# Cached keys of the sliding heads: one transfer of 512 KB for each chunk of four sequences

## Time and profile before

| what | value |
|---|---|
| median of 3 runs | 3058.83 us (3041.25 to 3075.09) |
| profiled execution, its own time | 3047.57 us |
| its span, from first to last instruction | 3045.9 us |
| PE busy | 2879.0 us, 95% of the span |
| PEld busy | 2334.0 us, 77% |
| DVE busy | 1530.6 us, 50% |
| ACT busy | 604.9 us, 20% |
| POOL busy | 174.2 us, 6% |
| mean granted TensorE clock | 0.974 of full |

### The profile page before, as it was taken

One profiled execution on the slowest core, in us unless ns is written; L12 is line 12 of the kernel. 1 busy time (PEld: TensorE's weight loads), 2 busy tenths in 40 slices (PEclk: granted clock), 3 DMA queues, 4 the chain that ended last, 5 costly groups with the idle time before them and its releaser, 6 DMA issues.

```text
span 3045.9 us, 45683 instructions
## 1 busy us (share of the span) xinstructions
PE 2879.0 (95%) x16270; PEld 2334.0 (77%) x16270; DVE 1530.6 (50%) x3125; ACT 604.9 (20%) x1279; POOL 174.2 (6%) x207
## 2 busy tenths in 40 slices
PE   7999999999898899999989999999898989999997
PEld 5888887878765678888778888778786657888885
DVE  5444537746655254445354454485475632544534
ACT  1000001124464210010010000112335641000000
POOL 3000000000142000000000000000003310000000
PEclk9999999999999899999999999999998999999998
DMA  7532222230279523322233312222205793233122
GB/s 162 140 83 71 60 77 80 73 101 0 82 238 272 155 76 83 83 69 63 73 104 83 83 55 82 71 84 70 74 0 175 232 264 110 70 83 83 52 78 67
DMA packets 366185, 301.35 MB, mean 99 GB/s; under 512 B 14738, under 2 KB 338540, under 8 KB 365842
## 3 DMA queue, kind: packets, MB, share of 16 engines
q1 hardware_dynamic: 341756, 217.98, 25.7%
q0 software_dynamic: 24256, 81.11, 8.9%
HBM read 287.21 MB, written 14.45 MB: 99 GB/s over the span
## 4 chain that ended last, share of the span: by engine, by line
PE 87%; DMA 4%; DVE 4%; issue 2%; ACT 2%; DVEq 1%; SPq 0%; ACTq 0%; POOL 0%; POOLq 0%
PE banks L731 34%; PE banks L824 18%; PE banks L756 5%; PE banks L767 5%; PE banks L695 4%; PE banks L1412 4%; PE banks L895 2%; PE banks L906 2%; PE banks L1090 2%; PE banks L1078 2%; PE banks L1094 2%; DMA arena<-in_cache_v,layer_cache_rows 1%; DMA keys_values_by_token<-in_w_gate 1%; PE banks L1307 1%; PE banks L1243 1%
## 5 line engine op out<-in xcount | busy, mean ns | idle before, releaser
L731 PE MATMUL banks<-normed_or_mixed,arena 128*128 128x272 f32 x1408 | 337.8, 393 | 4.5 <-DVE arena L1976 4.5
L731 PE MATMUL banks<-arena 128*128 128x272 f32 x1408 | 337.0, 392 | 0.0
L731 PEld LDWEIGHTS banks<-normed_or_mixed,arena 128*128 128x128 f32 x1408 | 266.9, 190 | 62.5 <-issue 4.1
L731 PEld LDWEIGHTS banks<-arena 128*128 128x128 f32 x1408 | 267.5, 190 | 55.1
L731 PE MATMUL banks<-arena,keys_values_by_token 128*128 128x272 f32 x832 | 204.4, 392 | 0.0
L731 PEld LDWEIGHTS banks<-arena,keys_values_by_token 128*128 128x128 f32 x832 | 158.1, 190 | 32.6
L824 PE MATMUL banks<-hidden_or_projected,keys_values_by_token 128*128 128x272 f32 x704 | 177.0, 392 | 0.0
L824 PE MATMUL banks<-arena,keys_values_by_token 128*128 128x272 f32 x704 | 169.6, 393 | 1.0 <-DVE arena L2033 1.0
L1490 ACT ACTIVATE hidden_or_projected<-banks 128x1024 f32<-128x1024 f32 (+4 forms) x160 | 130.9, 827 | 199.4 <-PE banks L695 122.7
L824 PE MATMUL banks<-hidden_or_projected,weight_slots 128*128 128x272 f32 x704 | 169.2, 392 | 0.0
L1974 DVE TENSOR_TENSOR arena<-arena,banks 128x272 f32<-128x272 f32 x88 | 38.4, 437 | 236.4 <-PE banks L731 236.4
(11 more groups left out here) (392 smaller groups left out, 4466.3 us busy)
## 6 DMA issues: line engine op xcount, KB each, us to landing
weight_slots<-in_w_down SPq DMA_DIRECT2D x128, 256.0 KB
weight_slots<-in_w_in SPq DMA_DIRECT2D x28, 1024.0 KB
keys_values_by_token<-in_w_gate SPq DMA_DIRECT2D x48, 512.0 KB, 5.0
keys_values_by_token<-in_w_up SPq DMA_DIRECT2D x48, 512.0 KB, 5.2
weight_slots<-in_w_gate SPq DMA_DIRECT2D x40, 512.0 KB, 5.0
weight_slots<-in_w_up SPq DMA_DIRECT2D x40, 512.0 KB, 5.1
hidden_or_projected<-in_cache_win_k SPq DMA_DIRECT2D x112, 128.0 KB, 6.4
weight_slots<-in_w_down SPq DMA_DIRECT2D x64, 192.0 KB
```

The source lines that it names most:

```text
L731: mm = pe.matmul(ps[:, bank, 0:HALF], weights[:, k, :], acts[:, k, :], start=first and k == 0, stop=k == 3, skip_group_check=True)
```

## The change

The four requests of a chunk are written as one: the source is taken over four sequences at once, four sequences x 32 rows x 4 KB, and the destination is the whole slot, 128 partitions x 4 KB. It adds 16 to the semaphore once. The counts that the users of `bk_in` wait for go down accordingly from 64 to 16 for each chunk. Nothing else is touched: the order of the requests on SP, the waits before them, the ring and TensorE's program are as they were.

```diff
@@ -408,12 +408,12 @@
             chunks = (CH_B + RING - 1 - slot) // RING
-            return s[f"bk_in{slot}"], l * (64 * chunks + 32) + 64 * chunks + (32 if m > 8 else 16)
+            return s[f"bk_in{slot}"], l * (16 * chunks + 32) + 16 * chunks + (32 if m > 8 else 16)
 
         def b_keys_in(l, m):
 
             chunks = (CH_B + RING - 1 - m % RING) // RING
-            return l * (64 * chunks + 32) + 64 * (m // RING + 1)
+            return l * (16 * chunks + 32) + 16 * (m // RING + 1)
@@ -558,13 +558,13 @@
                     i, g, slot = m // 2, m % 2, m % RING
                     sp.wait_ge(s["k_free"], k_seen(l, CH_C + m))
                     alone(sp)
-                    for b4 in range(4):
-                        rows = A["cache_win_k"][ds(l, 1), 4 * g + b4].rearrange("l p h d -> (l p) (h d)")
-                        if i < 4:
-                            src = rows[1536 + 128 * i:1664 + 128 * i].rearrange("(k r) c -> k r c", r=4)
-                        else:
-                            src = rows[512 * (i - 4):512 * (i - 3)].rearrange("(k r) c -> k r c", r=16)[:, 0:4, :]
-                        ld(k_rows_in[32 * b4:32 * b4 + 32, slot], src, f"bk_in{slot}")
+                    rows = A["cache_win_k"][ds(l, 1), 4 * g:4 * g + 4].rearrange("l b p h d -> (l b) p (h d)")
+                    if i < 4:
+                        src = rows[:, 1536 + 128 * i:1664 + 128 * i].rearrange("b (k r) c -> b k (r c)", r=4)
+                    else:
+                        src = rows[:, 512 * (i - 4):512 * (i - 3)].rearrange("b (k r) c -> b k r c", r=16)[:, :, 0:4, :]\
+                            .rearrange("b k r c -> b k (r c)")
+                    ld(k_rows_in[:, slot].rearrange("p r c -> p (r c)"), src, f"bk_in{slot}")
                 for m in range(2 * NB_S):
```

## The result

Four runs of the changed kernel have a median of 3118.86 us (3116.65 to 3125.82) against 3053.63 us for four runs of the kernel before, a ratio of 1.0211 with a 95% interval of 1.0181 to 1.0240. The forecast was 3128, with a range of its own of 3105 to 3150. The two medians lie 65.2 us apart. The profiled execution has a span of 3116.7 us, 70.8 us more than before; the forecast for both was 69 more.

The account below looks back on a forecast made before the run. PE bounds the kernel (busy 95%), with DMA engines nearly without reserve in the key stage. Four engines carrying keys plus values add 34.5 us per layer, 69 in all, to the 3058.83 median: 3128 us, range 3085 to 3205.

Parts of the forecast that it names:

- What bounds it, and what could be won: Whole kernel and B's key stage: PE sets the pace, DMA share 0.99; a better load could return 10.6 us, 0.35%.
- The requests that go: SP's queue: 56 requests per layer become 14, freeing 13.3 us at 0.316 us each, worth nothing by itself.
- How the one transfer is dealt out: Joined key request: outermost counts 4 against 128 give four engines, the same each time, 128 KB on each.
- a table of 34 rows: Set-up load at 0.13 share, 2.1 engines, 55 GB/s; taken as evidence that engines get equal shares of the outermost count.
- What four engines can carry: Key stage: each engine moves 2.523 MB at 23.6 GB/s, 106.9 us, so 34.5 us more per layer, 69 in all.
- my upper pace: Key stage: at 26.4 GB/s per engine the bytes take 95.6 us, 23.2 us more per layer, 46 in all.
- PE's own work lies wholly inside, also where its clock falls: Key stage: PE's 64.89 us of work fits inside the 110 us, with 35 us more to spare at a lower clock.
- What would show it: Expected signs: key waits about 35 us per layer, value waits gone, SP's stretch towards 95 us, rate near 185 GB/s.
- All sixteen engines: Joined key request is cut by its 128 destination rows; at most 10.6 us gained, 3048 us; chance 0.10.
- The ring hides it: Key stage: four engines, but requests go out 10 to 16 us ahead; 5.4 us late per layer, 3070; chance 0.08.
- The slow pace: Key stage: four engines at 15.9 GB/s, from two queues or the 2 MB distance; up to 173 us, 3232; chance 0.17.

Follow-up runs that it names:

- `sixteen`: Changed kernel with its single 512 KB request reordered to (row, sequence), outermost count 32; 3042.95 us, ratio 0.9952 to the kernel before.
- `by_row`: Kernel before with each chunk's four 128 KB requests taking one 1 KB row of all 128 partitions, outermost count 4; 3127.61 us.
- `pairs`: Kernel before with a chunk's four requests joined two and two, 256 KB each, outermost count 2; 3264.32 us.
- `novals_after`: Changed kernel with the last sixteen requests for C's values in each layer left out; 3066.89 us, against 3021.33 for the kernel before cut likewise.
- `quarters`: Kernel before with partitions ordered (row, sequence): four requests per chunk, 8 rows x 4 sequences onto 32 partitions, eight engines; 3066.72 us.
- `halves`: Kernel before with partitions ordered (row, sequence): two requests per chunk, 16 rows x 4 sequences onto 64 partitions, sixteen engines; 3045.34 us.
- `by_pool`: Changed kernel with the same key request, outermost count 4, asked for by POOL between its requests for values; 3098.87 us, ratio 1.0141.

## Why the prediction was right

**What bounds it, and what could be won.** Right, as far as it can be told. The stage had no DMA engine to spare, and only waits of 10.6 us could be won. `sixteen` takes the waits for keys away and shortens the stretches by 1.1 and 0.6 us. Its timed gain of 0.5% is more, some 14 us, though its interval, 9 to 20 us, holds the 10.6. Where the rest comes from is in part open. The profiles show it outside the stretch (2885.4 against 2892.7 us), where single profiles differ as much by themselves, and there is one profile of each. The timed runs say what goes with it: their mean granted clock is 0.9775 in the median with `sixteen` and 0.973 before, and among the runs before alone the one at 0.975 took 3047.27 us and the one at 0.968 took 3067.07, which by estimate makes 13 us for a difference of 0.0045. Part of it is the stage itself (0.98 and 0.96 in place of 0.93, and 0.92 in place of 0.83 in the 33 to 35 us behind it in the first layer); what lifts the rest isn't shown.

**The requests that go.** The direction was right, the price off: one request of the new form takes SP 0.556 us and not 0.316, so that 14 of them save 56 x 0.316 - 14 x 0.556 = 9.9 us per layer and not 13.3. It is worth nothing, as forecast: `by_row` has all 56 requests and is as slow.

**How the one transfer is dealt out.** Right, and shown three ways: 4.2 engines in the window in which only keys move; count 4 against 32 at equal size and number; two engines with `pairs`. The guess by analogy from a table of 34 rows on 2.1 engines held. The Trainium skill, "DMA: Bandwidth & Descriptors", under "Why a DMA increments its semaphore by 16 and not by 1", has the rule and says the lowest-numbered engines are taken on SP's queue, while POOL's rotates. No run here shows an engine's number, but that the load adds up on SP's queue (share 0.58) and spreads on POOL's (0.92) agrees.

**What four engines can carry.** Right within 4 us. From the first request at 918.05 to chunk 45 at 1031.67, less 2.65, each of the four moved 2.523 MB in 111.0 us: 22.7 GB/s, where I took 23.6, and 111.0 - 106.9 = 4.1 us is just the difference between 34.5 and 38.5. `pairs` gives 4.36 MB in 182.3 us, 23.9 GB/s. `novals_after`, with six requests for values in the stretch, gives 2.03 MB in 82.6 us, 24.6 GB/s. That bytes on a shared engine add up is what `novals_after` shows. With keys alone an engine is quicker (26.5), so my upper pace was real, but over a whole stretch the engines had 22.7 to 24.6. The pace of 23.6 that I took came from another mix, values alone on all sixteen engines; that it lies within 4% of 22.7 is partly luck. That the net of 70.8 lies so near to 69 is luck too, in part: 78 in the stretches, less 7.3 elsewhere.

**"PE's own work lies wholly inside, also where its clock falls."** This step was half wrong, at little cost. PE waited for keys for only 17.8 and 26.1 us, not about 35. The rest of the stretch went into slower work: PE's busy time rose by 18.9 and 15.6 us as the granted clock fell from 0.93 to 0.73. In the window 968 to 988 the clock is 0.50, the lower level of 1.2 GHz; before it PE had waited five times, 15.3 us, within 31. It didn't set the end here, because the engines went on filling the ring meanwhile: in windows of 4 us each, the share never fell under 0.25, that is four engines of sixteen, in either stretch. In `quarters`, where the engines ran out of work (0.02 above), it did cost time.

**What would show it.** The share under 0.99 and the rate near 185 came true (0.58, 184 and 181); SP's stretch went to 88 us, not 95. The waits for values didn't vanish: 8.6 and 5.4 us, where they had been 4.2 and 5.3. I take it that a chunk of values isn't in until its sixteenth on the same four engines is, behind the keys' packets; no run tries this by itself. In `pairs`, where PE waits 95.2 and 86.1 us for keys, it doesn't wait for values at all.

**The rivals.** *All sixteen engines:* excluded by `sixteen` against the changed kernel. The Trainium skill, "DMA: Bandwidth & Descriptors", under "Rules for kernel authors", advises one 128-partition transfer in place of two to halves of the partitions. Where the outermost count allows sixteen engines the runs agree weakly (`sixteen` had stretches of 75.3 and 76.2 us, `halves` 76.8 and 77.6), and where it doesn't, they contradict the advice: the joined request cost 2.1% (1.0211). *The ring hides it:* excluded; a request went out 10 to 16 us ahead, but chunk 45's took 26.3. It lost for the reason given, a cadence and not a latency. *The slow pace:* excluded for the four engines, whose pace was 22.7. But its cause, which I had placed in the mix of queues or the distance of 2 MB, was wrong as well: `sixteen` has both and runs at 348 GB/s per full share.

## What to carry to other kernels

When requests are joined, look at the outermost count of both sides and not at the size: with 16 and 32 the keys here were on all sixteen engines, with 8, 4 and 2 on that many, and with 34 on two; on SP's queue the loads piled up on the same few each time. A ring hides latency but not a rate: add up the bytes that the busiest DMA engine has to move in the stage, other queues' shares included, and compare with the steps. A DMA share well under 1 beside an engine that waits for a DMA is a sign of it (0.58 here, 0.99 before).

Before a wait is called harmless because another engine has time to spare, look at what it does to the granted clock: in `quarters` 4.2 us of waits for keys came with 5.7 us more busy time for the same products.

## What the runs showed of the hardware that was not expected

- *A busy DMA engine isn't always at the same pace.* Per full share the sixteen moved 276 GB/s with requests onto 32 partitions, 296 with 64 and 348 with 128, all on sixteen engines. `quarters`, with 32 partitions on eight engines, had 339, and `by_pool` only 225. `halves` and `quarters` both give an engine four partitions and differ, so the number of partitions on an engine isn't what counts. The rest fits the thought that two engines which write to the same group of partitions get into each other's way, which I gave as the theory for `halves`; but it was not tried by itself, and it stays a reading.
- *A step of four in the moving operand costs TensorE time:* a score product over 128 columns took 405 ns in the median in place of 273, while the same step in ACT's read of the banks cost nothing (1021 ns both ways).
- *A request can hold its sequencer:* SP's requests for keys took up to 3.5 us in the changed kernel and up to 10.8 us, 4.8 in the median, in `pairs`, against a median of 0.556 in the changed kernel and 0.538 in `sixteen`. What stood behind them on SP's queue were mostly requests for the same few engines, so it isn't shown to cost anything here.
